# Opening of a decoder layer: small rows issued by ScalarE, SyncE beginning with activations and modulation chunks, and the first projection chunk in two halves

## What is computed

```python
ada = silu(c) @ w_ada + b_ada                       # 6 modulation vectors for each of 9 conditionings
h = rms_norm(x, g_mix_pre) * (1 + scale1) + shift1
z = h @ w_in      # -> x_rnn | q | k | v | forget logits | gate_A | gate_B
y_A = rg_lru(causal_conv(x_rnn))                    # branch A: convolution and gated recurrence
y_B = forgetting_attention(q, k, v, logf)           # branch B: causal for the prompt, paged cache for samples
x = x + gate1 * rms_norm((sigmoid(g_A) * y_A + sigmoid(g_B) * y_B) @ w_out, g_mix_post)
h = rms_norm(x, g_ffn_pre) * (1 + scale2) + shift2
x = x + gate2 * rms_norm(moe_top4_of_32(h), g_ffn_post)
```

## Time and profile before

| | |
|---|---|
| time, three runs | 1373.33, 1373.27, 1370.23 us (median 1373.27) |
| profiled execution | 1372.02 us, of which the profile's span is 1370.3 |
| TensorE busy (matmul) | 1304.2 us, 95% |
| VectorE, ScalarE, GpSimd busy | 357.1, 207.7, 38.4 us |
| moved from HBM | 484.77 MB, 358 GB/s over the span |
| chain that ended last | TensorE 65%, DMA 30% |

### The profile page before, as it was taken

One profiled execution on the slowest core, in us unless ns is written; L12 is line 12 of the kernel. 1 busy time (PEld: TensorE's weight loads), 2 busy tenths in 40 slices (PEclk: granted clock), 3 DMA queues, 4 the chain that ended last, 5 costly groups with the idle time before them and its releaser, 6 DMA issues.

```text
span 1370.3 us, 15525 instructions
## 1 busy us (share of the span) xinstructions
PE 1304.2 (95%) x6186; PEld 580.5 (42%) x6186; DVE 357.1 (26%) x754; ACT 207.7 (15%) x475; POOL 38.4 (3%) x79
## 2 busy tenths in 40 slices
PE   5999999999999999999999999999999999999896
PEld 2656466655463433434344342334334343343332
DVE  2542225766452121112122111211211122121122
ACT  2124424411221100101011010101101010010101
POOL 1100002000020000000000000000000000000000
PEclk9999999999989999999999999999999999999998
DMA  9836586789676999999999999999999999999993
GB/s 345 285 141 266 185 281 173 208 230 260 233 281 242 414 428 428 428 428 427 427 426 428 428 427 428 401 426 425 428 428 429 428 422 429 428 427 428 427 427 137
DMA packets 71905, 491.06 MB, mean 358 GB/s; under 512 B 11814, under 2 KB 24862, under 8 KB 44053
## 3 DMA queue, kind: packets, MB, share of 16 engines
q1 hardware_dynamic: 68564, 480.86, 86.9%
q0 software_dynamic: 3264, 9.13, 2.5%
HBM read 484.77 MB, written 5.18 MB: 358 GB/s over the span
## 4 chain that ended last, share of the span: by engine, by line
PE 65%; DMA 30%; DVE 2%; issue 1%; SPq 1%; ACT 0%; DVEq 0%
PE bank L1949 29%; DMA ring<-in_w_gate_up_dram 27%; PE bank L1632 8%; PE bank L1658 4%; PE bank L1937 3%; PE bank L2016 2%; PE bank L1620 2%; PE bank L1506 2%; PE bank L1787 2%; PE bank L1913 2%; DMA ring<-in_w_in_dram 1%; PE bank L1572 1%; PE bank L1914 1%; PE bank L2044 1%; PE bank L1940 1%
## 5 line engine op out<-in xcount | busy, mean ns | idle before, releaser
L1949 PE MATMUL bank<-ring,work 128*64 128x512 f32 x1984 | 439.9, 597 | 11.2 <-issue 5.9
L1949 PEld LDWEIGHTS bank<-ring,work 128*64 128x64 f32 x1984 | 155.2, 137 | 281.7 <-issue 281.7
L1949 PE MATMUL bank<-ring,hT 128*64 128x512 f32 x896 | 206.2, 608 | 14.1 <-DMA ring<-in_w_gate_up_dram 14.1
L1449 DVE TENSOR_TENSOR gbT<-gbT,bank 128x512 f32<-128x512 f32 x80 | 55.0, 688 | 436.6 <-PE bank L1940 301.6
L1949 PEld LDWEIGHTS bank<-ring,hT 128*64 128x64 f32 x896 | 69.1, 139 | 148.6 <-issue 148.6
L1632 PE MATMUL bank<-hT,ring 128*128 128x320 f32 x384 | 106.8, 439 | 2.1 <-DMA ring<-in_w_in_dram 2.1
L1405 DVE TENSOR_SCALAR work<-bank 128x512 f32<-128x512 f32 x32 | 22.0, 687 | 317.9 <-PE bank L1949 299.1
L1632 PEld LDWEIGHTS bank<-hT,ring 128*128 128x128 f32 x384 | 73.3, 192 | 36.3 <-issue 5.9
L1658 PE MATMUL bank<-hT,ring 128*128 128x320 f32 x256 | 73.6, 437 | 0.2 <-ACT gaT L705 0.2
L1937 PE MATMUL bank<-work 128*128 128x512 f32 x128 | 67.8, 631 | 0.0
L842 ACT ACTIVATE work<-bank 128x320 f32<-128x320 f32 x15 | 6.6, 438 | 394.0 <-PE bank L1506 394.0
(11 more groups left out here) (375 smaller groups left out, 913.0 us busy)
## 6 DMA issues: line engine op xcount, KB each, us to landing
ring<-in_w_gate_up_dram SPq DMA_DIRECT2D x128, 2048.0 KB, 16.0
ring<-in_w_down_dram SPq DMA_DIRECT2D x64, 2048.0 KB, 17.3
ring<-in_w_ada_dram SPq DMA_DIRECT2D x12, 2048.0 KB, 10.6
ring<-in_w_in_dram SPq DMA_DIRECT2D x12, 2048.0 KB, 11.0
ring<-in_cache_k_dram SPq DMA_DIRECT2D x64, 128.0 KB, 6.6
ring<-in_cache_v_dram SPq DMA_DIRECT2D x16, 512.0 KB, 6.4
ring<-in_w_out_dram SPq DMA_DIRECT2D x2, 2048.0 KB, 12.7
out_dram<-tok POOLq DMA_DIRECT2D x2, 1024.0 KB, 8.5
```

The source lines that it names most:

```text
L1449: TTo(piece(gbf, i), piece(gbf, i), B[6 + n % 2][:, :], ALU.add).then_inc(s["scatter_read"], 1)
L1949: last = mm(bank[CAP * x:CAP * x + CAP, :], lhsT[:, CAP * x:CAP * x + CAP], rhs(x), start=start, stop=stop)
```

## The change

SyncE begins with x and goes on with chunks 0 to 3 without anything between. The three conditioning rows become the first instructions of ScalarE's block, before the sigmoid and its wait for `vec_made`. The twelve small issues come on ScalarE right behind the sigmoid and before the wait for x and the squares. Chunk 4 is issued as two transfers of 1 MB, tiles 0 to 3 of the contraction with the semaphore of its place, tiles 4 to 7 with `c_in`; in the first projection job TensorE waits for `c_in` at 64 before the fifth tile. Nothing is left out and no byte is added.

```diff
+        FIRST_W = 4
 ...
         @block.sync
         def _(eng):
-            def tiles(v, o="(t p)"):
-                return v.rearrange("o (t p) -> (o t) p", p=128)
-
             def chunk(c):
                 if c >= 4:
                     consumer, n = FREED[c - 4 if c < 7 else c - 3]
                     eng.wait_ge(s[consumer], n)
-                eng.dma_start(staged(c, CHUNKS[c].shape[1]), CHUNKS[c]).then_inc(chunk_in[stage(c)], 16)
-
-            for at_, v in ((48, c_prompt), (56, c_sample), (0, b_ada)):
-                rows = v.shape[0] * v.shape[1] // 128
-                eng.dma_start(vrows[at_:at_ + rows, 1, :], tiles(v)).then_inc(s["c_in"], 16)
+                w_ = staged(c, CHUNKS[c].shape[1])
+                if c == FIRST_W:
+                    for h in range(2):
+                        eng.dma_start(w_[:, 4 * h:4 * h + 4, :], CHUNKS[c][:, 4 * h:4 * h + 4, :])                            .then_inc(s["c_in"] if h else chunk_in[stage(c)], 16)
+                else:
+                    eng.dma_start(w_, CHUNKS[c]).then_inc(chunk_in[stage(c)], 16)
+
             eng.dma_start(tok[:, 0:2, :], x_prompt[0].rearrange("(t p) n -> p t n", p=128)).then_inc(s["x_in"], 16)
             eng.dma_start(tok[0:NS, 2, :], x_sample.rearrange("b q n -> (b q) n")).then_inc(s["x_in"], 16)
             chunk(0)
-            for at_, v in ((0, g_mix_pre), (8, g_mix_post), (16, g_ffn_pre), (24, g_ffn_post), (32, conv_b),
-                           (40, rg_b_a), (48, rg_b_x), (56, rg_lambda), (64, conv_w[0])):
-                rows = v.shape[0] * NT
-                eng.dma_start(vrows[at_:at_ + rows, 0, :], tiles(v)).then_inc(s["rows_in"], 16)
-            eng.dma_start(vrows[0:64, 2, :], tiles(state_h[0])).then_inc(s["rows_in"], 16)
-            scv = state_conv[0].rearrange("b j (t p) -> (b j t) p", p=128)
-            for i in range(2):
-                eng.dma_start(vrows[0:96, 3 + i, :], scv[96 * i:96 * i + 96, :]).then_inc(s["rows_in"], 16)
-
 ...
         @block.scalar
 ...
-
+            def tiles(v, o="(t p)"):
+                return v.rearrange("o (t p) -> (o t) p", p=128)
+
+            for at_, v in ((48, c_prompt), (56, c_sample), (0, b_ada)):
+                rows = v.shape[0] * v.shape[1] // 128
+                eng.dma_start(vrows[at_:at_ + rows, 1, :], tiles(v)).then_inc(s["c_in"], 16)
             eng.wait_ge(s["vec_made"], 1)
             A_(sigc, vec("c", NR * NT), ACT.Sigmoid).then_inc(s["csig_made"], 1)
+
+            for at_, v in ((0, g_mix_pre), (8, g_mix_post), (16, g_ffn_pre), (24, g_ffn_post), (32, conv_b),
+                           (40, rg_b_a), (48, rg_b_x), (56, rg_lambda), (64, conv_w[0])):
+                rows = v.shape[0] * NT
+                eng.dma_start(vrows[at_:at_ + rows, 0, :], tiles(v)).then_inc(s["rows_in"], 16)
+            eng.dma_start(vrows[0:64, 2, :], tiles(state_h[0])).then_inc(s["rows_in"], 16)
+            scv = state_conv[0].rearrange("b j (t p) -> (b j t) p", p=128)
+            for i in range(2):
+                eng.dma_start(vrows[0:96, 3 + i, :], scv[96 * i:96 * i + 96, :]).then_inc(s["rows_in"], 16)
 
             eng.wait_ge(s["x_in"], 32)
 ...
         @block.tensor
 ...
                     for k in range(NT):
                         if j == 0:
+                            if k == 4:
+                                eng.wait_ge(s["c_in"], 64)
                             eng.wait_ge(s["h_made"], k + 1)
```

## The result

The changed kernel takes 1376.63 us in the median of 20 runs (1372.87 to 1381.03), against 1371.97 (1369.36 to 1375.41) for the kernel before in 20 runs beside it. The ratio is 1.0032 with a 95% interval of 1.0023 to 1.0041: 4.4 us slower by the ratio, where 2.5 us faster was forecast. The profiled execution has a span of 1375.5 us, 5.2 above the one before. One execution of experiment 9 took 1519.74 us, at a mean granted clock of 0.845 where the others had 0.986 to 0.991, and is left out of its ratio.

The account below looks back on a forecast made before the run. TensorE was taken as busy almost throughout, idling only in the opening behind SyncE's stream. The first job's end gained 2.5 us: 1372.0 - 2.5 = 1369.5 profiled, 1370.8 for the median with 1.25 us added; range 1367.3 to 1374.8.

Parts of the forecast that it names:

- Where the time is decided: Between 42 and 460 us nobody on TensorE waits for a transfer, so a gain before 42 us carries through whole.
- Activations first: SyncE's opening: x and chunk 0 issued 1.8 us earlier; chunk 0 lands at 12.5, chunk 3 at 29.4.
- Conditioning rows on ScalarE: ScalarE's start: three issues covered by idle time; rows beside x delayed 0.7 us, 1.2 at most; sigmoid ends at 5.8.
- Twelve issues on ScalarE: Behind the sigmoid: twelve issues take 5.0 us, so squares start at 10.8, eating 0.5 of the 1.8 us.
- The rival of a full queue: ScalarE stalls in an issue before the squares: one stall 0.5 us slower, two 3.9 us; chance 0.08.
- The rule of the rivals: First job's end: squares + 5.5 gives turn of x, + 17.8 first tile, + 5.9 end, against 42.9 before.
- second failed step: TensorE from the turn of x to the end of chunk 2 takes 12.96 us without a pause.
- Small rows, when they land: Before TensorE's chunk 2: 352 small rows land at 13 to 18 us, needed at 26.2; cover 8 us.
- The trickle rival: Small rows wait for several chunk rows each, landing at 39, with TensorE held before chunk 2: 10 us slower, 1383; chance 0.05.
- Halves: First projection chunk in two transfers: first half there at 32.2, h decides at 34.2; worth 0 to 0.5 us.
- What would show it wrong: Squares later than 12, TensorE waiting for small rows, chunk 3 not moving, or the 2.5 us missing at 450.
- my cases: Outcomes weighed: forecast gain 0.53, ScalarE issues at GpSimd's price 0.20, faster 0.14, full queue 0.08, trickle 0.05.

Follow-up runs that it names:

- experiment 9: Kernel before with SyncE reordered to x, conditioning rows, chunk 0, twelve small issues, chunks 1 to 3; projection chunk in halves; nothing on ScalarE: ratio 0.9979.
- experiments 2: Changed kernel with the twelve small issues back on SyncE behind chunk 0, only the conditioning rows on ScalarE: ratio 0.9987 to the kernel before.
- the second trace: Changed kernel, unchanged, executed again for another profile: 1378.94 us, first job read at 49.55.
- Experiment 4: Changed kernel plus twelve unread identity products on TensorE between chunk 0 and the turn of x: ratio 1.0011 to the kernel before.
- Experiments 7: Changed kernel with the twelve small issues on ScalarE moved behind the squares and the root: ratio 1.0016 to the kernel before.
- 8: Changed kernel with small issues on ScalarE behind squares and root, and conditioning rows on SyncE behind x: ratio 1.0005 to the kernel before.
- 10: SyncE order x, conditioning rows, chunk 0, small issues, chunks 1 to 3, nothing on ScalarE, projection chunk whole: ratio 0.996 to the kernel before.
- `c_first_on_sync`: Changed kernel with the three conditioning rows back at the front of SyncE's list, small issues still on ScalarE: ratio 0.999 to the kernel before.
- `sync_waits_for_c`: Changed kernel with SyncE waiting until the conditioning rows have landed before issuing x and everything behind: 1373.91 us, executed once.
- `reordered_whole_again`: Repeat of the reordered SyncE kernel with the projection chunk whole, unchanged: ratio 0.9987 to the kernel before, first job read at 44.44.
- `whole_chunk`: Changed kernel with the first projection chunk in one transfer and without TensorE's extra wait: ratio 1.0047 to the kernel before.
- `sync_reordered_warm`: Reordered SyncE kernel with halves, plus ten unread identity products before the conditioning rows are turned and six before chunk 0: ratio 0.9964 to the kernel before.

## Why the prediction was wrong, point by point

- *Where the time is decided*: right, as far as single traces tell. Nothing between 42 and 430 us absorbed the shift (381.5 and 382.6 us there before, 382.3 and 382.6 after). The opening lost 5.4 us and the runs 4.4.
- *Activations first*: right. Chunk 0 at 12.38 (12.5 forecast), no wait for chunk 3. In the traces of experiments 2 and 9 the 1.8 us reach the first job as 2.5 and 2.9; the ratio of 2 reaches to 1.0001, that of 9 excludes no change.
- *Conditioning rows on ScalarE*: **this step failed**. I let them be 0.7 us late, 1.2 at most, from eight turns against 4 KB rows of x. They were 5.2 us late, 6.8 in the second trace. The count assumed that a queue with new work gets its turn at once; from 3 to 5 us it got none, and then shared with chunk 0 until 8.5. I had a row that pointed the other way and read it for the small rows only: GpSimd's transfers landed 4.7 to 6.7 us after issue while SyncE's queue was full. Taken as the price for the conditioning rows it gives 2.8 + 4.7 to 6.7, landing at 7.5 to 9.5 (9.1 to 10.7 in the six traces). That was the nearest row, and an upper bound of 1.2 us beside it was too narrow.
- *Twelve issues on ScalarE*: right in size, 4.8 us (5.0 forecast), never stuck. The rival of a full queue was wrong in its mechanism: no single issue on ScalarE took more than 0.71 us. Its rule (slower from squares later than 13.7) held, for squares at 14.8.
- *The rule of the rivals*: squares + 5.46 = 20.27, as forecast. Then squares + 5.5 + 17.8 + 5.9 gives 44.0, 1.1 us behind the kernel before. Measured was 48.3. The missing 4.3 is the **second failed step**: I took TensorE's 12.96 us from the turn of x on as fixed, and it was 17.4, at half pace in the two groups above (4.5 us). I had priced the clock for the first job and not for idle time that a late ScalarE would open in front of the turn of x. Three of three traces in which TensorE had stood idle for 4.3 us or more there show a turn of 7.14 us; of fourteen without such idle time, two do. Experiment 4 takes the idle time away and the 4.5 us go. So idle time brings the half pace here, but it isn't its only cause.
- *Small rows, when they land*: wrong as well, hidden by the delay before it. The turns are what I took them for, one small packet for one large (182 to 184), but I counted 22 of them for each engine where 480 packets make 30, and they take until about 25.5 us in the changed kernel, 11 us behind the last issue (18 us was forecast as the latest). TensorE wanted them at 34.7, so it cost nothing. Experiments 7 and 8 uncover it: 2.5 us of wait and the clock behind it. The trickle rival had this place, with a size too large.
- The Trainium skill ("DMA: Bandwidth & Descriptors", Queues, rings and completion order) has each DMA engine alternate between its queues by packets of typically 9 to 17 descriptors. Where small rows stood beside 8 KB rows, the trace doesn't agree: nine such rows would hold an engine for 2.8 us (an estimate, from 418/16 GB/s), but in windows of 0.1 us the two queues' packets already stand side by side, 7 and 7 from 18.7 to 18.8 us. For the silence from 3 to 5 us, when x's 20 rows for each engine pass without one of the other queue's, such a turn would be an explanation; no run here shows the mechanism.
- *Halves*: 0 to 0.5 us fits (0.5 us of the first job between 9 and 10, nothing in the ratios).
- *What would show it wrong*: the first sign named there, squares later than 12, is what came.

The range failed with these two. Neither conditioning rows this late nor the clock behind a new idle time stood in any of my cases, though both had rows: the earlier trace rows.

## What to carry to other kernels

A small transfer that the critical path waits for doesn't get faster by a queue of its own once another queue is full: price it by the landing of small transfers under load, not by its bytes and not by the issues it saves. Put it behind the first large transfer of the same queue (here x, 1.25 MB) and before the megabytes that nobody waits for yet: in experiment 9 TensorE was on chunk 0 at 12.50 all the same (12.38 in the changed kernel), and this order has the lowest ratios of all that were tried, 0.996 to 0.9987. And when a path gets a new idle time of several microseconds on TensorE, have a case in which the work behind it goes at half pace; here that was about 10 us of it.

## What the runs showed of the hardware that I had not expected

- A transfer of 60 KB in ScalarE's queue is there 1.6 us behind its last issue alone (4.26), 5.0 behind it with x in SyncE's queue (7.77), 6.3 to 7.9 with chunks behind x (9.1 to 10.7).
- Small packets of one queue and 8 KB rows of another pass one for one, about 46 of each in a microsecond over the 16 DMA engines, so the 480 packets of the 352 small rows need some 10 us and more, however few bytes they are.
- TensorE's half pace isn't tied to idle time alone. In `c_first_on_sync` the granted clock fell to 0.50 at 29.5 us with TensorE busy since 14.5; in `sync_waits_for_c` and `reordered_whole_again` the turn of x took 7.14 us right behind chunk 0 while the granted clock read 1.00, as it did in `whole_chunk` behind 4.4 us of idle time. In every trace chunk 0, the first larger work, took 3.3 to 3.6 us where later chunks took 1.9 at full pace, and except in `sync_reordered_warm` its windows too read 1.00. Half pace in the turn of x and in chunk 1 makes 3.6 of the 3.8 us by which the two executions of the reordered opening differ (40.6 and 44.4). What sets it where TensorE wasn't idle, no run here shows.
